# Hybrid encoder trunk on one core: the first pooling group turned round, and no multiplications of constants ahead of it

## The reference, cut to what matters

```
y = xf * lax.rsqrt(jnp.mean(xf * xf, axis=-1, keepdims=True) + EPS);  return y * g     # rms_norm
for g, w in enumerate(POOL_WINDOWS):                                                    # 2, 4, 8, 16
    hg = hf[..., g * POOL_GROUP:(g + 1) * POOL_GROUP]
    cs = jnp.cumsum(hg, axis=1)
    lagged = jnp.pad(cs, ((0, 0), (w, 0), (0, 0)))[:, :s]
    groups.append((cs - lagged) / cnt - hg)
y = jnp.einsum('bsgc,gce->bsge', pooled, w_pool).reshape(b, s, d);  return y * scale
h = h + multiscale_pool_mixer(rms_norm(h, mix_norm[l]), pool_w[l], pool_scale[l])
h = h + sqrelu_mlp(rms_norm(h, mlp_norm[l]), w_mlp_in[l], w_mlp_out[l])
```

## Time and profile before

| | |
|---|---|
| median of 3 runs | 1809.44 us (1809.17 to 1809.59) |
| the profiled execution: its own time | 1808.98 us |
| its span, first to last instruction | 1807.2 us |
| TensorE busy | 1798.6 us, 100% of the span |
| VectorE busy | 1436.0 us, 79% |
| ScalarE busy | 992.4 us, 55% |
| DMA | 348.55 MB, 193 GB/s over the span |

### The profile page before, as it was taken

The page is one execution under the profiler, slowest core; times in us unless marked ns, Lnnn a source line. Parts: engine busy times, 40 slices in busy tenths (PEclk is TensorE's granted clock), DMA queues, the critical chain, the costliest instruction groups (busy, mean ns, idle before and its releaser), DMA issues.

```text
span 1807.2 us, 23220 instructions
## 1 busy us (share of the span) xinstructions
PE 1798.6 (100%) x8200; PEld 1492.9 (83%) x8200; DVE 1436.0 (79%) x1481; ACT 992.4 (55%) x1099; POOL 13.0 (1%) x17
## 2 busy tenths in 40 slices
PE   9999999999999999999999999999999999999998
PEld 7888888888888888888888888888888888888887
DVE  7898978888887976755557776898888879797966
ACT  7665656464655554643445545664646555565643
POOL 0000000000000000000000000000000000000000
PEclk9999999999999999999999999999999999999999
DMA  8465655564746475566564446465647464645671
GB/s 316 157 209 184 230 187 209 186 221 156 254 159 233 140 256 159 181 193 188 186 192 151 132 161 225 148 209 187 219 157 256 159 233 139 232 169 204 213 253 70
DMA packets 178643, 348.55 MB, mean 193 GB/s; under 512 B 10624, under 2 KB 10752, under 8 KB 178176
## 3 DMA queue, kind: packets, MB, share of 16 engines
q1 hardware_dynamic: 177984, 346.02, 56.7%
q10 hardware_dynamic: 576, 1.44, 0.2%
HBM read 345.32 MB, written 2.10 MB: 192 GB/s over the span
## 4 chain that ended last, share of the span: by engine, by line
PE 99%; issue 0%; DVE 0%; ACT 0%; DVEq 0%; POOLq 0%; POOL 0%
PE bank L1492 25%; PE bank L1494 25%; PE bank L1493 25%; PE bank L1457 6%; PE bank L1459 6%; PE bank L1458 6%; PE bank L1518 1%; PE bank L1484 1%; PE bank L1721 1%; PE bank L1809 0%; PE bank L1736 0%; PE bank L1808 0%; PE bank L1738 0%; PE bank L1856 0%; PE bank L1854 0%
## 5 line engine op out<-in xcount | busy, mean ns | idle before, releaser
L1492 PE MATMUL bank<-w_hi,u_hi_a 128*128 128x512 f32 x896 | 348.7, 389 | 0.0
L1494 PE MATMUL bank<-w_hi,u_lo_a 128*128 128x512 f32 x896 | 348.6, 389 | 0.0
L1493 PE MATMUL bank<-w_lo,u_hi_a 128*128 128x512 f32 x896 | 348.6, 389 | 0.0
L1492 PE MATMUL bank<-w_hi,mix_hi 128*128 128x512 f32 x684 | 267.8, 391 | 0.2
L1494 PE MATMUL bank<-w_hi,mix_lo 128*128 128x512 f32 x684 | 266.2, 389 | 0.0
L1493 PE MATMUL bank<-w_lo,mix_hi 128*128 128x512 f32 x684 | 266.2, 389 | 0.0
L548 ACT ACTIVATE w_hi<-arena 128x2048 fp32r<-128x2048 f32 x100 | 191.6, 1916 | 130.1 <-PE bank L1494 99.9
L910 DVE TENSOR_TENSOR w_lo<-arena,w_hi 128x2048 fp32r<-128x2048 f32 x100 | 227.7, 2287 | 39.8 <-ACT w_hi L548 39.7
L560 ACT ACTIVATE w_hi<-raw 128x1024 fp32r<-128x1024 f32 x112 | 119.1, 1063 | 179.9 <-PE bank L1494 170.0
L541 ACT ACTIVATE w_hi<-raw 128x1024 fp32r<-128x1024 f32 x128 | 133.6, 1062 | 148.4 <-PE bank L1459 142.4
L898 DVE TENSOR_TENSOR w_lo<-raw,w_hi 128x1024 fp32r<-128x1024 f32 x128 | 153.4, 1222 | 72.9 <-ACT w_hi L541 72.3
(11 more groups left out here) (203 smaller groups left out, 2783.0 us busy)
## 6 DMA issues: line engine op xcount, KB each, us to landing
raw<-in_w_mlp_in SPq DMA_DIRECT2D x128, 512.0 KB, 4.7
arena<-in_w_mlp_in SPq DMA_DIRECT2D x128, 512.0 KB, 5.3
raw<-in_w_mlp_out SPq DMA_DIRECT2D x128, 512.0 KB, 6.0
arena<-in_w_mlp_out SPq DMA_DIRECT2D x128, 512.0 KB, 5.1
raw<-in_w_kv SPq DMA_DIRECT2D x64, 512.0 KB, 4.4
raw<-in_w_q SPq DMA_DIRECT2D x32, 512.0 KB, 4.6
raw<-in_w_o SPq DMA_DIRECT2D x32, 512.0 KB, 4.2
raw<-in_pool_w SPq DMA_DIRECT2D x4, 512.0 KB, 9.7
```

The costliest lines, as they stand in the source:

```text
L1492: nc.tensor.matmul(bank[:], hi, w_hi[:, slot, kk, :], start=begin, stop=False)
L1493: nc.tensor.matmul(bank[:], hi, w_lo[:, slot, kk, :], start=False, stop=False)
L1494: return nc.tensor.matmul(bank[:], lo, w_hi[:, slot, kk, :], start=False, stop=end)
```

## The change

Four things are different.

- `keep_busy` and its tile are gone: TensorE issues nothing until data have landed.
- Group 0 is turned round. TensorE first transposes the unscaled x of its 512 columns (eight transposes), ACT and DVE split that with the gain, `pool_group(0)` multiplies it by the weights, ACT copies the product out with the row scale `rms` (two activations of 128x512, `product_rows`), and three float32 matmuls of 512 columns with the unscaled band of group 0 pool it (`bands_of_first`). TensorE's order is transposes, group 0, bands 1, the bands of the first, bands 2, group 1, bands 3, group 2, `turn_h`, group 3, `turn_h`.
- The DMAs are put in another order and cut in another way. SP issues x (rows 0, columns 0 to 512), one half each of the weight halves 0 and 1, x (rows 0, 512 to 1536), x (rows 0, 1536 to 2048), the bands, weight halves 2 to 7, the column scale. ACT issues x (rows 1, 0 to 512), identity and gains, the other halves of weight halves 0 and 1, x (rows 1, 512 to 1536) and x (rows 1, 1536 to 2048).
- DVE and ACT follow: splits of group 0 stand ahead of the rest of the squares, the bands of groups 1 to 3 alone are scaled, and the splits 5, 6 and 7 on DVE come later, 6 and 7 of them between `pool_add(0)` and `pool_add(1)`.

```
-X_ACT = [(0, slice(0, 1024), 0), (1, slice(0, 512), 0), (1, slice(1024, 1536), 2)]
-X_DVE = [(0, slice(1024, D), 1), (1, slice(512, 1024), 1), (1, slice(1536, D), 3)]
+X_ACT = [(0, slice(SW, 3 * SW), 1), (1, slice(SW, 3 * SW), 1)]
+X_DVE = [(0, slice(0, SW), 0), (1, slice(0, SW), 0), (0, slice(3 * SW, D), 2), (1, slice(3 * SW, D), 2)]
...
+            load_x(X_DVE[0], x_dve_landed[0])
+            for n in range(2):
+                sp.dma_start(raw[:, n, 0], pool_view[0, 0][:, 2 * n, :]).then_inc(raw_landed[n], 16)
             load_x(X_ACT[0], x_act_landed[0])
-            load_x(X_ACT[1], x_act_landed[1])
-            load_x(X_ACT[2], x_act_landed[2])
             load_x(X_DVE[2], x_dve_landed[2])
-            sp.dma_start(pool_land, pool_consts).then_inc(pool_landed, 16)
+            sp.dma_start(pool_keep, pool_consts).then_inc(pool_landed, 16)
...
+            load_x(X_DVE[1], x_dve_landed[1])
+            act.dma_start(keep[:, 0:C_MASK], keep_consts[:, 0:C_MASK]).then_inc(head_landed, 16)
+            for n in range(2):
+                act.dma_start(raw[:, n, 1], pool_rows[:, 2 * n + 1, :]).then_inc(second_landed[n], 16)
+            load_x(X_ACT[1], x_act_landed[1])
+            load_x(X_DVE[3], x_dve_landed[3])
...
+            act.wait_ge(head_landed, 16)
+            for n in range(2):
+                pooled_to_hi(0, n)
+                pool_split(n)
...
+            act.wait_ge(pe_done, 2)
+            for tb in range(TB):
+                nc.scalar.activation(product_rows[:, tb], PAIR[1][tb][:], ACT.Copy, scale=rms[:, 0, tb:tb + 1]).then_inc(rows_copied, 1)
...
             for b in range(2):
                 pooled_to_lo(2, b)
+            pool_split(5)
+            dve.wait_ge(scale_landed, 16)
             pool_add(0)
+            pool_split(6)
+            pool_split(7)
             pool_add(1)
...
-            pe.wait_ge(warm_set, 1)
-            keep_busy(8)
+            pe.wait_ge(head_landed, 16)
+            for i in range(2):
+                pe.wait_ge(x_dve_landed[i], 16)
+            for b in range(2):
+                for c in (2 * b, 2 * b + 1):
+                    for tb in range(TB):
+                        at = (c % 2) * SEQ + tb * P
+                        last = nc.tensor.transpose(pooled_bank(0, b)[:, at:at + P], h[:, tb, c * P:(c + 1) * P], ident)
+                last.then_inc(band_done, 1)
...
+            def bands_of_first():
+
+                pe.wait_ge(rows_copied, TB)
+                nc.tensor.matmul(PAIR[0][0][:], bands[:, 0, 0:P], product_rows[:, 0], start=True, stop=True)
+                nc.tensor.matmul(PAIR[0][1][:], bands[:, 0, REACH:], product_rows[:, 1], start=True, stop=False, skip_group_check=True)
+                nc.tensor.matmul(PAIR[0][1][0:REACH - P, :], bands[:, 0, P:REACH], product_rows[:, 0],
+                                 start=False, stop=True, skip_group_check=True).then_inc(first_pooled, 1)
+
+            pool_group(0)
             pe.wait_ge(band_first, 1)
             pe.wait_ge(band_second, 1)
-            pool_bands(0)
-            pe.wait_ge(band_first, 3)
             pool_bands(1)
-            for g in range(NG):
-                pool_group(g)
...
+            pe.wait_ge(pool_landed, 16)
+            bands_of_first()
+            pool_bands(2)
+            pool_group(1)
+            pool_bands(3)
+            pool_group(2)
+            turn_h(0, 0, 1)
+            pool_group(3)
+            turn_h(0, 1, 2)
```

More of the change, by code:

```diff
@@ L84 @@
 X_O = NG
-C_IDENT, C_MASK, C_COS, C_SIN = 0, P, P + 384, P + 384 + TB * 4 * ROT
+G_MIX, G_MLP, G_KV, G_SUB, G_ROWS = 0, 32, 64, 80, 82
+C_IDENT, C_GAIN = 0, P
+C_MASK = C_GAIN + G_ROWS
+C_COS = C_MASK + 384
+C_SIN = C_COS + TB * 4 * ROT
 C_END = C_SIN + TB * 4 * ROT
@@ L145, in trunk @@
         keep = sb("keep", [P, C_END])
-        gain = sb("gain", [P, G_ROWS])
+        gain = keep[:, C_GAIN:C_GAIN + G_ROWS]
         sub_gain = sb("sub_gain", [P, 2])
@@ L252, in trunk @@
         sums_cleared = sem("sums_cleared")
-        ident_landed = sem("ident_landed")
+        head_landed = sem("head_landed")
+        second_landed = [sem(f"second_landed{i}") for i in range(2)]
+        rows_copied = sem("rows_copied")
+        first_pooled = sem("first_pooled")
         keep_landed = sem("keep_landed")
@@ L393, in load_pool @@
             def load_pool(source):
-                for n in range(HALVES):
+                for n in range(2, HALVES):
                     sp.dma_start(raw_half[n // RAW][:, n % RAW], source(n // 2, n % 2)).then_inc(raw_landed[n], 16)
@@ L754, in mlp, with load_x @@
                                                      accum_out=ssq[:, 4, tb, g:g + 1]).then_inc(last_squared, 1)
-            for i in range(2):
-                tb, cols, _ = X_DVE[i]
-                act.dma_start(h[:, tb, cols], x[0, tb * P:(tb + 1) * P, cols]).then_inc(x_dve_landed[i], 16)
+            def load_x(piece, landed):
+                tb, cols, _ = piece
+                act.dma_start(h[:, tb, cols], x[0, tb * P:(tb + 1) * P, cols]).then_inc(landed, 16)
+            pool_rows = pool_w.rearrange("l g (c p) n -> l g p c n", p=P)[0, 0]
+            load_x(X_DVE[1], x_dve_landed[1])
[4 more added lines that the diff above has]
+            load_x(X_DVE[3], x_dve_landed[3])
             act.wait_ge(sums_cleared, 2)
             nc.scalar.activation(x_ssq[:, :, 4:5], x_ssq[:, :, 4:5], ACT.Copy).then_inc(sums_cleared, 1)
[L762 to L765, removed]
             def pool_split(n):
                 act.wait_ge(raw_landed[n], 16)
+                if n < 2:
+                    act.wait_ge(second_landed[n], 16)
                 nc.scalar.activation(w_hi[:, n], raw_half[n // RAW][:, n % RAW], ACT.Copy).then_inc(hi_ready, 1)
@@ L776, in pooled_to_hi @@
                                          scale=gain[:, G_MIX + kt:G_MIX + kt + 1]).then_inc(pooled_hi, 1)
+            act.wait_ge(head_landed, 16)
+            for n in range(2):
+                pooled_to_hi(0, n)
+                pool_split(n)
+            for i, (tb, cols, slot) in enumerate(X_ACT):
+                act.wait_ge(x_act_landed[i], 16)
+                nc.scalar.activation(squares[:, tb, cols], h[:, tb, cols], ACT.Square, scale=D ** -0.5,
+                                     accum_out=x_ssq[:, tb, slot:slot + 1]).then_inc(x_act_squared, 1)
             act.wait_ge(pool_landed, 16)
             act.wait_ge(rms_done, 1)
[L780 to L785, removed]
-            pool_split(2)
-            pooled_to_hi(1, 0)
+            nc.scalar.activation(bands[:, 1:NG, REACH:], bands[:, 1:NG, REACH:], ACT.Copy, scale=rms[:, 0, 1:2]).then_inc(band_second, 1)
+            pool_split(2)
+            act.wait_ge(pe_done, 2)
+            for tb in range(TB):
+                nc.scalar.activation(product_rows[:, tb], PAIR[1][tb][:], ACT.Copy, scale=rms[:, 0, tb:tb + 1]).then_inc(rows_copied, 1)
+            for b in range(2):
+                pooled_to_hi(1, b)
             pool_split(3)
-            pooled_to_hi(1, 1)
-            for n in range(4, HALVES):
+            pool_split(4)
+            for b in range(2):
+                pooled_to_hi(2, b)
+            for n in range(5, HALVES):
                 pool_split(n)
             for g in range(NG):
-                if g + 2 < NG:
-                    pooled_to_hi(g + 2, 0)
-                    pooled_to_hi(g + 2, 1)
+                if g == 1:
+                    for b in range(2):
+                        pooled_to_hi(3, b)
                 if g >= 1:
@@ L1151, in mlp, with x_squares @@
                         split(S_KV, g)
-            nc.vector.memset(warm_tile, 1.0).then_inc(warm_set, 1)
             dve.wait_ge(sums_cleared, 2)
-            for i, (tb, cols, slot) in enumerate(X_DVE):
+            def x_squares(i):
+                tb, cols, slot = X_DVE[i]
                 dve.wait_ge(x_dve_landed[i], 16)
@@ L1184, in pooled_to_lo @@
                                                    hi.bitcast(F32), ALU.mult, ALU.subtract).then_inc(pooled_lo, 1)
[L1186 to L1189, removed]
+            for i in range(2):
+                x_squares(i)
+            dve.wait_ge(head_landed, 16)
+            for n in range(2):
+                pooled_to_lo(0, n)
+                pool_split(n)
+            for i in range(2, 4):
+                x_squares(i)
+            dve.wait_ge(x_dve_squared, len(X_DVE))
+            dve.wait_ge(x_act_squared, len(X_ACT))
+            dve.wait_ge(sums_cleared, 3)
+            nc.vector.tensor_reduce(mean[:, 0, :], x_ssq[:], AX.X, ALU.add).then_inc(mean_done, 1)
+            dve.wait_ge(pool_landed, 16)
+            dve.wait_ge(rms_done, 1)
+            nc.vector.tensor_scalar(bands[:, 1:NG, 0:REACH], bands[:, 1:NG, 0:REACH], rms[:, 0, 0:1], None, ALU.mult).then_inc(band_first, 1)
+            nc.vector.tensor_scalar(sub_gain[:], gain[:, G_SUB:G_SUB + 2], 1.0 - LAM_INIT, None, ALU.mult).then_inc(gains_ready, 1)
             pool_split(2)
-            pooled_to_lo(1, 0)
```

(29 more changed lines are left out.)

22 lines of the change are left out of this document (3 added, 19 removed).

## The result

The changed kernel takes **1811.84 us** (median of 22 runs, 1811.28 to 1812.78) against 1809.30 us (22 runs, 1808.93 to 1809.59): 2.5 us longer, a ratio of 1.0014 with an interval from 1.0008 to 1.0020. That is within 0.2% of no change and within the range of the prediction (1808.4 to 1812.6), but 1.3 us beyond its point and 0.2 us outside the forecast's own narrower range (1809.4 to 1811.6). The runs also spread more: 1.50 us from the fastest to the slowest, where the kernel before has 0.66.

A forecast was written before the change was run, and what follows sets the result against it. TensorE was taken as the bound from 11.56 us on. Group 0 from 9.4 to 17.6 plus 26.34 put the MLP at 43.94 instead of 42.85: 1809.44 + 1.1 = 1810.5 us, range 1808.4 to 1812.6.

The forecast's parts named there:

- the forecast's own narrower range: Whole kernel: 1809.4 to 1811.6 us if the main forecast holds, which was given a chance of 0.60.
- What bounds it: From 11.56 us TensorE alone is the chain; the kernel's end moves as much as the MLP's first matmul.
- rival B: MLP's second block: DVE becomes the bound and TensorE waits 1.4 us; +2.5 us, 1811.9; chance 0.14.
- The start of group 0: Group 0's first product, set by data landing and splits: claimed at 9.4 us, estimate 8.8 to 10.8.
- Going back from 6.01 at the pace of that queue: Landing of identity and gains behind 363 KB of ACT's queue: 4.8 us reckoned, 5.1 taken.
- The norm's bands: Before bands 1: scaled bands claimed ready at 14.6 us, 3 us before TensorE wants them.
- rival C: First weight half lands late, at 10.1, and group 0 starts at 12.5; +4.2 us, 1813.6; chance 0.07.
- The time at the low level: Group 0's products: low clock for 5.9 us from 9.4, each us costing 0.47; group 0 ends at 17.6.
- Rival A: Group 0: clock rises at 11.0, as transposes and idle time don't reset the count; -0.9 us, 1808.5; chance 0.16.
- The new work: Between group 0 and MLP: three float32 matmuls add 2.58 us; MLP starts 26.34 us after group 0 ends.
- DVE: MLP's second block: `pool_add(3)` ends at 46.6, TensorE wants it at 46.7; no loss counted.
- The sum: Whole kernel: MLP start moves from 42.85 to 43.94, 1.1 us later; median 1809.44 + 1.1 = 1810.5 us.

The follow-up runs named there:

- e3: The changed kernel with the first weight half split ahead of the transposed x on ACT and DVE; 3.75 us over the kernel before.
- e6: The changed kernel with all DMAs but the first x pieces, identity and gains held back until identity and gains landed; 3.65 us over the kernel before.
- e9: The changed kernel with constants before transposes and before group 0, rounded-part pooling, identity and gains ahead of x; 1.27 us over the kernel before.
- e1: The kernel before without its multiplications of constants, nothing else changed; 1.85 us over the kernel before, ratio 1.0010.
- e7: The changed kernel with the first group's product pooled by six matmuls of rounded parts after bands 2, not three float32; 2.00 us over the kernel before.
- e2: The changed kernel with three multiplications of ones before the transposes and three before group 0; 1810.51 us, 1.38 over the kernel before.
- e10: e9 with weight halves 2 and 3 split earlier on ACT and DVE; 1809.17 us against 1809.03 for the kernel before, ratio 1.0001.
- e5: The changed kernel with three multiplications of ones before the transposes and none before group 0; 2.62 us over the kernel before.
- e8: The changed kernel with constants before the transposes only, rounded-part pooling, identity and gains ahead of x on ACT's queue; 1.37 us over the kernel before.

## Why the prediction was right, and where it was off

**What bounds it: right.** All but 0.2 us of the change shows in where the MLP's first matmul stands, the rest takes the same time, and after 11.23 TensorE never waits. The measured 1811.84 is all but the 1811.9 of rival B; that is chance, as B did not happen.

**The start of group 0: the step that failed.** "Going back from 6.01 at the pace of that queue" took a landing to follow the bytes ahead in its own queue, and gave 5.1 us for identity and gains, 6.9 for the first weight half and 9.4 for group 0. Measured were 6.8, 8.65 (e3) and 11.23, beyond the 10.8 of the bound. e6 shows a reason for the first: what is issued behind shares the way. There is a second, which stays open: from 2 to 5 us the changed kernel moved 0.70 MB, and the kernel before 0.99. The term is 1.8 us too small. The norm's bands, 14.6 reckoned and 16.8 measured, were early by a like mistake: the last piece of x was taken at 12.0 with the bytes ahead of it on both queues (3.1 MB) and without those behind, and DVE got it at 14.3, when 4.4 MB had moved. The 3 us to spare were 2.1. Of the rival C, which had the weights as the late ones at 10.1, only the direction came true: in e3 they landed at 8.65, and in the changed kernel ACT took them at 8.77 without a wait. In e9, where ACT's turn comes earlier, it waited 0.33 us for them, until 8.64.

**The time at the low level: right in kind, too long.** 5.9 us taken, 4.2 measured, in other traces 3.4 (e1) to 5.3 (e6, e7). Group 0 took 7.67 us, not 8.2: 0.5 too much. That the clock costs what it was said to, e1 shows directly (3.4 x 0.47 = 1.6 us, 1.65 in its trace). Kernels with group 0 or bands 0 at the low level spread by 1.1 us and more and those kept busy (e2, e9, e10) by 0.3 to 0.5 in about as many runs; with 0.47 us lost for each us at the low level, a spread of 1.5 us would be 3 us between the earliest and the latest rise (an estimate, as the runs themselves have no trace). So one profiled rise is probably a sample, and the one row that I took, 5.9 us, was the longest of all traces.

**Rival A (the transposes and the idle time leave the count alone)** wanted a rise 5.9 us after the transposes, at 12.7 with their real start; it came at 15.4. Whether they helped at all stays open.

**The new work: mechanism right, size 0.3 us low.** 26.34 us were reckoned from the end of group 0 to the MLP, 26.67 measured. The three matmuls cost 2.9 us rather than 2.58: the last takes 0.96 in place of 0.86 and the pair behind it 0.44 instead of 0.25.

**DVE: right, with luck in the margin.** Nothing was counted and nothing was lost; the margin was 0.7 us, 0.1 reckoned. Rival B did not happen in the changed kernel, but it was the next bound: in e9 it took 0.6 us at the MLP's first block as soon as TensorE was early; e10 removed this wait, and not the 0.3 us at the second block.

**The sum.** 1.09 + 1.83 (start) - 0.53 (clock) + 0.33 (pooling) = 2.72 us for the MLP's start, as measured, and 0.2 at the end of the kernel that no step foresaw.

## What to carry to other kernels

Starting the dense engine earlier gains nothing if the early work runs at the low clock and needs extra work to be undone: price both before moving it. Multiplications of no use can earn their place while the engine has nothing else, and also in a gap in the middle. Reckon the landing of a first transfer from everything issued close to it, on all queues and behind it too, and treat a clock's rise seen in one profile as one of several possible.

## What the runs showed of the hardware that I had not expected

- The clock fell in the midst of products: after an idle stretch of 3.3 us (e5) they began at 0.23 us each at 11.14, went to 0.43 at 12.5, and were back at 0.23 at 16.0. In e8 the same happened at 12.5 and 15.9. The Trainium skill, "TensorE: Matmul & The Clock Gate", "HAM oscillation — how this bites in real kernels", says that an idle gap brings the engine back to half rate, so that the next work starts slow. The trace agrees on the loss and not on the moment: the work began at the high level, and the loss came 1.3 us after it had resumed.
- The first piece of x, 256 KB on SP's queue, landed at 5.6 us with everything behind it issued and at 4.8 with that held back (e6); in the kernel before the first pieces had 512 KB and were there at 5.7 and 6.0: halving a piece gained far less than half.
- 7.5 in place of 7.2 us between the last matmul and the end of the span, in all ten traces of the changed start and not in that of e1; nothing in the change touches that part of the code. I have no reason for it.
